# Crossing the queries of three head groups by DMA in a two-block float32 transformer kernel

## What is computed

```python
q, k, v, gate, qi, ki, wi = split_cols(h @ w_in, A_WIDTHS)
q = rope(rms_norm(q.reshape(B, T, N_HEADS, HEAD_DIM), q_g), pos)
k = rope(rms_norm(k.reshape(B, T, N_KV_HEADS, HEAD_DIM), k_g), pos)
...
logits = jnp.einsum('bqgrd,bqkgd->bqgrk', qb, k_sel).astype(jnp.float32) * scale
p = jax.nn.softmax(logits, axis=-1).astype(v.dtype)
o = jnp.einsum('bqgrk,bqkgd->bqgrd', p, v_sel)
...
return (jax.nn.silu(gate) * o) @ w_out
```

## Time and profile before

| what | value |
|---|---|
| median of 3 runs | 2251.98 us (2251.95 to 2251.99) |
| the profiled execution | 2252.53 us |
| its span on the core | 2251.2 us |
| PE busy | 2232.7 us |
| DVE busy | 1384.7 us |
| ACT busy | 1211.2 us |
| POOL busy | 88.7 us |
| granted TensorE clock, mean | 0.999 |

### The profile page before, as it was taken

The page is one execution under the profiler, slowest core; times in us unless marked ns, Lnnn a source line. Parts: engine busy times, 40 slices in busy tenths (PEclk is TensorE's granted clock), DMA queues, the critical chain, the costliest instruction groups (busy, mean ns, idle before and its releaser), DMA issues.

```text
span 2251.2 us, 28162 instructions
## 1 busy us (share of the span) xinstructions
PE 2232.7 (99%) x11490; PEld 1842.5 (82%) x11490; DVE 1384.7 (62%) x1860; ACT 1211.2 (54%) x1638; POOL 88.7 (4%) x81
## 2 busy tenths in 40 slices
PE   9999999999999999999999999999999999999998
PEld 7888888888888888888788888888888888888886
DVE  5677765757665675675665556765555455554555
ACT  5556675655665664554454555565444344534444
POOL 0003210003220000000000000000000000000000
PEclk9999999999999999999999999999999999999999
DMA  7456676656686653545644456677666566656663
GB/s 273 147 170 178 192 215 219 206 168 192 189 240 208 189 165 118 164 132 167 208 150 150 150 168 207 221 217 221 199 205 206 187 199 207 210 187 195 197 206 112
DMA packets 300898, 424.11 MB, mean 188 GB/s; under 512 B 108577, under 2 KB 108737, under 8 KB 300641
## 3 DMA queue, kind: packets, MB, share of 16 engines
q1 hardware_dynamic: 298608, 415.20, 58.4%
q0 software_dynamic: 1584, 6.16, 1.0%
q10 hardware_dynamic: 576, 0.95, 0.1%
HBM read 396.06 MB, written 2.10 MB: 177 GB/s over the span
## 4 chain that ended last, share of the span: by engine, by line
PE 96%; DVE 2%; ACT 1%; issue 1%; DMA 0%; ACTq 0%; DVEq 0%
PE ACC L990 29%; PE ACC L992 29%; PE ACC L991 29%; ACT arena L1019 1%; PE SCPV L585 1%; DVE WL L2083 1%; PE TP L532 0%; ACT WH L1019 0%; PE TP L507 0%; PE SCPV L592 0%; PE SCPV L727 0%; PE SCPV L584 0%; PE SCPV L593 0%; PE SCPV L594 0%; PE SCPV L721 0%
## 5 line engine op out<-in xcount | busy, mean ns | idle before, releaser
L2083 DVE TENSOR_TENSOR WL<-W,WH 128x1024 fp32r<-128x1024 f32 x740 | 910.1, 1232 | 613.6 <-ACT WH L1019 612.2
L1019 ACT ACTIVATE WH<-W 128x1024 fp32r<-128x1024 f32 x740 | 780.6, 1056 | 798.1 <-PE ACC L992 791.8
L990 PE MATMUL ACC<-WH,XH 128*128 128x512 f32 x2592 | 1041.3, 402 | 4.3 <-ACT arena L1019 3.1
L992 PE MATMUL ACC<-WH,XL 128*128 128x512 f32 x2592 | 1011.4, 390 | 0.0
L991 PE MATMUL ACC<-WL,XH 128*128 128x512 f32 x2592 | 1009.5, 389 | 0.0
L990 PEld LDWEIGHTS ACC<-WH,XH 128*128 128x128 f32 x2592 | 487.0, 188 | 113.9 <-DVE WL L2083 5.2
L992 PEld LDWEIGHTS ACC<-WH,XL 128*128 128x128 f32 x2592 | 486.5, 188 | 104.5
L991 PEld LDWEIGHTS ACC<-WL,XH 128*128 128x128 f32 x2592 | 487.5, 188 | 95.2 <-issue 1.0
L990 PE MATMUL ACC<-WH,HH 128*128 128x512 f32 x328 | 128.8, 393 | 0.0
L992 PE MATMUL ACC<-WH,HL 128*128 128x512 f32 x328 | 127.7, 389 | 0.0
L991 PE MATMUL ACC<-WL,HH 128*128 128x512 f32 x328 | 127.7, 389 | 0.0
(11 more groups left out here) (308 smaller groups left out, 1319.4 us busy)
## 6 DMA issues: line engine op xcount, KB each, us to landing
W<-in_w_in SPq DMA_DIRECT2D x84, 1024.0 KB, 5.0
W<-in_a_w_in SPq DMA_DIRECT2D x47, 1024.0 KB, 5.4
W<-in_w_ffn_gate SPq DMA_DIRECT2D x44, 1024.0 KB, 5.2
W<-in_w_ffn_up SPq DMA_DIRECT2D x44, 1024.0 KB, 5.4
W<-in_w_ffn_down SPq DMA_DIRECT2D x44, 1024.0 KB, 5.1
W<-in_b_w_in SPq DMA_DIRECT2D x40, 1024.0 KB, 5.2
W<-in_a_w_out SPq DMA_DIRECT2D x16, 1024.0 KB, 5.8
W<-in_b_w_out SPq DMA_DIRECT2D x16, 1024.0 KB, 6.4
```

Source lines behind the costliest of these rows:

```text
L990: MM(out, hx, WH[:, k, 0:ch.width], start=q == 0 and k == 0, stop=False)
L992: ins = MM(out, lx, WH[:, k, 0:ch.width], start=False, stop=last and k == QK - 1)
L1019: return nc.scalar.activation(out, in_, func, **how)
L2083: TT(tiles_of(M.WL[K.pair(n)], ch, half), tiles_of(M.W[n % 4], ch, half), tiles_of(M.WH[K.pair(n)], ch, half).bitcast(F32), ALU.subtract). ...
```

## The change

For groups 1 to 3 of "a" and "b" the queries are no longer transposed by PE. POOL splits them into halves (`query_halves`, two copies of 128x1024 16-bit values), SP issues one DMA transpose (`cross_queries`), and POOL joins the halves into QT (`queries_joined`, two copies). Group 0 stays as it was. PE passes three empty steps in place of the transposes and waits for `queries_joined` ahead of the first scores; ACT no longer copies TP into QT for these groups. In POOL's order the split of the next group's queries stands between the split and the join of the first pair's probabilities in groups 1 and 2 (in group 0 behind the split of the second pair), and the join of the queries stands ahead of the join of the second pair (in group 0 behind it). The rooms HALVES[l] and CROSSED[l] are shared with the gated outputs, so the first crossing of these ("go", c = 0) begins 11 instead of 2 visits after its gate product, with waits for the last queries. Of the two `attend` hunks the first is PE's and the second ACT's; `halves` of ACT and DVE get a wait for `queries_crossed` of group 3 where SP's `cross` waits for `queries_joined`. The new functions of the last hunk are POOL's, and its `halves` and `joined` are the splitting and joining of probabilities as before.

```diff
+        for g in range(1, NKV):
+            begin(after(l + ".q0") + (24, 41, 66)[g - 1], "queries_cross", l, g)
         for c in range(3):
-            begin(after(f"{l}.g{c}") + 2, "halves", "go." + l, c)
+            begin(after(f"{l}.g{c}") + (11 if c == 0 else 2), "halves", "go." + l, c)
...
     def cross(key, c):
+        if key[:2] == "go" and c == 0:
+            sp.wait_ge(*at("queries_joined", key[3], NKV - 1))
...
+    def cross_queries(l, g):
+        sp.wait_ge(*at("query_halves", l, g))
+        sp.dma_start_transpose(M.CROSSED[l], M.HALVES[l].rearrange("p u t w -> p (u t w)")).then_inc(*did("queries_crossed", l, g, by=16))
...
     def attend(l, g):
-        pe.wait_ge(*at("queries_roped", l, g))
-        yield from queries_transposed(l, g, M.Q)
-        yield
-        pe.wait_ge(*at("queries_turned", l, g, 1))
-        pe.wait_ge(*at("keys_turned", l, 1))
+        if g:
+            yield
+            yield
+            yield
+            pe.wait_ge(*at("queries_joined", l, g))
+        else:
...
     def attend(l, g):
-        yield from queries_turned(l, g, M.att[0])
+        if g:
+            yield
+            yield
+        else:
+            yield from queries_turned(l, g, M.att[0])
...
+        def query_halves(g):
+            x = M.Q[:, :, g * CH:(g + 1) * CH].bitcast(U16).rearrange("p t (w u) -> p t w u", u=2)
+            pool.wait_ge(*at("queries_roped", l, g))
+            if l == "a" and g == 1:
+                pool.wait_ge(*at("index_scored", IH - 1))
+            for u in range(2):
+                ins = pool.tensor_copy(M.HALVES[l][:, u], x[:, :, :, u])
+            ins.then_inc(*did("query_halves", l, g))
+
+        def queries_joined(g):
+            pool.wait_ge(*at("queries_crossed", l, g))
+            pool.wait_ge(*at("scores_multiplied", l, g - 1, GRP - 1))
+            q = M.att[0].bitcast(U16).rearrange("p k (t q u) -> p k t q u", t=TB, u=2)
+            for u in range(2):
+                ins = pool.tensor_copy(q[:, :, :, :, u], M.CROSSED[l][:, TB * QK * u:TB * QK * (u + 1), :].rearrange("p (t k) q -> p k t q", t=TB))
+            ins.then_inc(*did("queries_joined", l, g))
+
         for g in range(NKV):
+            halves(g, 0)
+            if 1 <= g < NKV - 1:
+                query_halves(g + 1)
+            joined(g, 0)
+            halves(g, 1)
+            if g == 0:
+                query_halves(1)
+                joined(g, 1)
+                queries_joined(1)
+                continue
+            if g < NKV - 1:
+                queries_joined(g + 1)
+            joined(g, 1)
```

More of the change, by code:

```diff
@@ L446, in sp_program @@
                 crossings.setdefault((visit + 1) // 4 + 5, []).append((visit, cross, args))
+            if name == "queries_cross":
+                crossings.setdefault((visit + 1) // 4 + 5, []).append((visit, cross_queries, args))
             if name == "attend":
@@ L572, in attend @@
         QT, LG, PR, PT = M.att
-        pe.wait_ge(*at("queries_roped", l, g))
-        yield from queries_transposed(l, g, M.Q)
-        yield
-        pe.wait_ge(*at("queries_turned", l, g, 1))
-        pe.wait_ge(*at("keys_turned", l, 1))
+        if g:
[4 more added lines that the diff above has]
+        else:
+            pe.wait_ge(*at("queries_roped", l, g))
+            yield from queries_transposed(l, g, M.Q)
+            yield
+            pe.wait_ge(*at("queries_turned", l, g, 1))
+            pe.wait_ge(*at("keys_turned", l, 1))
         v = lambda t: M.V[:, t, g * HD:(g + 1) * HD]
@@ L1039, in halves @@
         act.wait_ge(*at(*ready(c)))
+        if key[:2] == "go" and c == 0:
+            act.wait_ge(*at("queries_crossed", key[3], NKV - 1))
         A(own[:, 0], x[:, :, :, 0], ACT.Copy).then_inc(*did("low_halves", key, c))
@@ L1515, in halves @@
         dve.wait_ge(*at(*ready(c)))
+        if key[:2] == "go" and c == 0:
+            dve.wait_ge(*at("queries_crossed", key[3], NKV - 1))
         V.tensor_copy(own[:, 1], x[:, :, :, 1]).then_inc(*did("high_halves", key, c))
@@ L2131, in probs_turned, with halves @@
         whole, turned = M.PROBS.bitcast(U16).rearrange("p (w u) -> p w u", u=2), M.PROBS_TURNED.bitcast(U16).rearrange("p (n u) -> p n u", u=2)
-        for g in range(NKV):
[L2133 to L2145, removed]
+        def halves(g, p):
+            pool.wait_ge(*at("probs_exponentiated", l, g, 2 * p + 1))
+            for u in range(2):
+                ins = pool.tensor_copy(M.PROB_HALVES[:, u, :], whole[:, :, u])
+            ins.then_inc(*did("prob_halves", l, g, p))
@@ new lines, in joined @@
+        def joined(g, p):
+            pool.wait_ge(*at("probs_crossed", l, g, p))
+            if p:
+                pool.wait_ge(*at("outputs_multiplied", l, g, 2 * p - 1))
+            elif g:
+                pool.wait_ge(*at("outputs_multiplied", l, g - 1, GRP - 1))
+            for u in range(2):
+                ins = pool.tensor_copy(turned[:, :, u], M.PROBS_CROSSED[:, 6 * u:6 * u + 6, :].rearrange("p n q -> p (n q)"))
+            ins.then_inc(*did("probs_joined", l, g, p))
+        def query_halves(g):
[3 more added lines that the diff above has]
+                pool.wait_ge(*at("index_scored", IH - 1))
+            for u in range(2):
+                ins = pool.tensor_copy(M.HALVES[l][:, u], x[:, :, :, u])
+            ins.then_inc(*did("query_halves", l, g))
@@ new lines, in queries_joined @@
+        def queries_joined(g):
+            pool.wait_ge(*at("queries_crossed", l, g))
+            pool.wait_ge(*at("scores_multiplied", l, g - 1, GRP - 1))
+            q = M.att[0].bitcast(U16).rearrange("p k (t q u) -> p k t q u", t=TB, u=2)
+            for u in range(2):
+                ins = pool.tensor_copy(q[:, :, :, :, u], M.CROSSED[l][:, TB * QK * u:TB * QK * (u + 1), :].rearrange("p (t k) q -> p k t q", t=TB))
+            ins.then_inc(*did("queries_joined", l, g))
+        for g in range(NKV):
+            halves(g, 0)
[11 more added lines that the diff above has]
+            joined(g, 1)
```

## The result

The changed kernel takes 2257.06 us (median of 14 runs, 2255.61 to 2259.23) where the kernel before, run beside it, takes 2252.01 (14 runs, 2251.41 to 2252.61). The ratio is 1.0022 [1.0016, 1.0029]: slower by 5.05 us, where 5.2 us less were forecast (2246.8, in a range of 2246.0 to 2250.8). The profiled execution took 2256.3 us, with a span of 2255.0 and a granted clock of 0.999, so the clock has no part in what its trace shows. It has a small part in the median: the six of the 14 runs with a granted clock of 0.999 have a median of 2256.3 us, and the other eight, with 0.997 or 0.998, took 2256.09 to 2259.23. With 0.999 the change costs some 4.3 us.

What follows compares the result with a forecast made beforehand. PE, busy 99% of the span, was taken as the bound. 5.3 + 0.4 - 0.6 - 0.1 + 0.2 = 5.2 us gained, putting the median at 2246.8 us, in a range of 2246.0 to 2250.8.

Steps and rivals of the forecast that it cites:

- What the change takes away: Savings on PE and ACT: 5.3 us of transposes, 0.4 us of waits at group 1's first scores, nothing for ACT's copies.
- rival 2: POOL's query copies cost much more than scaled, making joins late at the values products: slower, about 2262 us; chance 0.05.
- The packets: PE's query transposes in groups 1 to 3: twelve packets of four removed, 0.44 us each, 5.3 us gained.
- Rival 5: Query transposes on PE: their full durations are the price, 13.1 us gained, 2239 us; chance 0.01.
- Group 0, second join: POOL's second join of probabilities, behind the split of group 1's queries: ends at 190.1, covered by about 0.4 us, cost 0.
- rival 1: POOL loses turns to DVE: PE waits at second joins of groups 0 and 2; gain only 2.6 us, 2249.4; chance 0.30.
- Group 1's first scores: Joined queries ready at 194.3 to 196.3, PE wants them at 197.5: cost 0, cover 1.2 us.
- Group 2, second join: Group 3's query joins delay POOL's join of probabilities: PE's wait grows 0 to 1.1 us per mixer.
- The late weight rest of "a": PE's late weight load: moved gated-output work gains up to 0.7 us, group 3's query splits may lose 0.9; +0.2 taken.
- SP: Six more transposes, 1.9 us each, on SP's queue; weight loads leave some 4 us later but are planned ahead: cost 0.
- Rival 3: Crossings land late, 7.1 us instead of 4.3, so PE waits at group 1's joins and others: 2249 to 2250; chance 0.08.

Runs made afterwards that it cites:

- the kernel with the third step: The changed kernel with a third empty step (yield) for ACT in groups 1 to 3, as many as before the change: 2248.49 us, ratio 0.9984.
- the move alone: The kernel before with only the first crossing of the gated outputs begun 11 visits after its gate product in place of 2: 2251.06 us, ratio 0.9995.
- the kernel whose median is 2254.68: The changed kernel, but PE transposes and ACT copies queries as before; added POOL copies and crossings stay, their result unread: 2254.68 us, ratio 1.0013.

## Why the prediction was wrong

**The step that failed** is one clause of "What the change takes away": "ACT also loses 12 copies, which are worth nothing, as it is 54% busy". The prediction put the term at nothing by ACT's busy share, and did not ask what the code in place of the copies does to ACT's order. Three yields stood around them, and the diff, which the prediction had before it, leaves two. That costs 8.6 us in the changed kernel (2257.06 against 2248.49; 7.8 with a granted clock of 0.999 in both) and 7.45 in the kernel before. A busy share can't show this: ACT idles for some 1000 us in sum, and has no slack at the two visits where a wait or a table load gets between a product and the take that frees its ACC. None of the rivals held it either; rival 2, the one on the slower side, named the length of POOL's copies, and those came as estimated.

**The sum itself** belongs to the kernel with the third step: 2248.49 against 2246.8, 1.7 us off. Point by point:

- The packets: 12 x 0.44 = 5.3 us. PE gains 0.44 and 0.36 us at the two packets of each group, 4.8 in all. The first scores of group 1 gain 0.30 in each mixer where 0.2 was put, and follow at the pitch:

```profile
197.06 0.39 PE L1008 MATMUL ACC<-WH,XL 128*128 128x512 f32 x1
197.29 0.38 PE L600 MATMUL SCPV<-arena 128*128 128x128 f32 x2
```

  Together 5.4 us read from the trace where 5.7 was put, and 6.2 by the medians. Rival 5 (13.1 us) is out, and the pitch was the right price.
- Group 0, second join. The two splits ended at 186.90, not 187.2, and the joins at 189.88, where 190.1 was put; PE comes at 190.44 and waits for nothing. The order in which POOL and DVE take turns came out as worked from the rows, and rival 1 fell at this place:

```profile
182.95 3.95 POOL L2179 COPY arena<-arena 128x1024 uint16<-128x1024 uint16 x2 [2.33 <-DVE arena L1612]
186.85 3.03 POOL L2170 COPY arena<-arena 128x768 uint16<-128x768 uint16 x2
191.33 3.58 POOL L2187 COPY arena<-arena 128x1024 uint16<-128x1024 uint16 x2 [1.45 <-DMA arena<-arena]
```

- Group 1's first scores: joined at 191.33 + 3.58 = 194.91, inside the 194.3 to 196.3 put; no wait.
- Group 2, second join: 0.6 us in "a" and 0.1 in "b" were put; with the third step 0.69 and 0.84 were lost. In "b" it was sized near the wrong end. The range itself was worked out unevenly: a query join that ends at 269.2 and 3.0 us of joining give 272.2, not 272.8. In the run the join of probabilities took 3.46.
- The late weight rest of "a": +0.2 was put for gain and loss together. The gain is 0.68 to 0.73 us, as the move alone shows; the splits of group 3 then take 0.43 in "a" and, what was not put, most of 0.72 in "b" (0.23 is left when they move).
- SP: "so 0" was wrong. The crossings cost 1.6 us together where PE still transposes. Rival 3 named the mechanism, a landing near 7 us (it was 6.8), and was given 0.08. The cost came at visit 54, the values product of group 1's second pair, whose probability crossing stands behind the late crossing of queries. What they cost with the third step alone no run shows.

Of the 3.6 us that copies and crossings cost by the medians, the sum held 1.2 (0.6 and 0.1 at the joins, 0.5 inside the +0.2); 2.4 were missed. In the trace with the third step the same places make 2.7 us (0.43, 0.69, 0.72, 0.84). The Trainium skill (Perfetto Trace Analysis, Optimizing Scalar/DVE Operations) warns that moving work between GpSimd and DVE may not pay, as they share a port. The rows bear the port out, one turn of about 1 us at most copies, and the copies' 2.0 us of cost; but as the work left PE, 6.2 us stand against it, and the rule didn't decide the sign. That 6.2 by the medians is 0.8 over the 5.4 of the trace has a reason in part: the kernel whose median is 2254.68 loses 2.0 us at visit 54 that the one with the third step doesn't, and does not lose the latter's 1.56 in "b". These give 0.5; the rest is near what the medians can tell.

## What to carry to other kernels

When a diff takes an engine's instructions out of a hand-made order, count the steps (yields, visits) that go with them, on each engine on both sides of the diff: one visit, early or late, on an engine that is 54% busy cost this kernel about 8 us. Look at which functions alternate there, since here an activation that needs another table cost two loads of 1.28 us where it fell between two that share one. And cost a shared port by the turns at the joins that someone waits for, not by its sum: two changes of POOL's order, one of them into its idle time, brought the median from 2248.49 to 2245.55 with not one instruction less.

## What the runs showed beside this

- A DMA transpose issued 1.5 us behind a 1 MB load held SP for 4.73 us and landed after 6.8, against 1.3 to 1.9 and 4.3 to 4.7 for the other query crossings of the changed kernel (those of group 1 came 4.8 us behind a load). With the transpose ahead of the load it was 1.98 and 4.32, and the next one paid part of it.
- The 12 splitting and 12 joining copies of 1024 columns in the changed kernel come in two lengths each, alone or with one turn: 1.04 or 2.0 us, 1.35 or 2.3. With the third step two of the 24 lie between (1.09 and 1.23). POOL lost no more than one turn for any copy.
- The spread from run to run goes with the granted clock. Of the changed kernel's runs the six with 0.999 took 2255.61 to 2257.03 us and the five with 0.997 took 2257.36 to 2259.23; the kernel before, 0.999 in all 27 runs beside the first experiments, had a median of 2251.99. Two of the twelve traces show a fall to 1.2 GHz ahead of the span's end, behind waits of PE for ACT of 1.92 and 2.34 us; other waits of that length had none behind them. Whether the other slow runs lost the clock at the same waits was not traced.
